# Seven block products, not eight, for three of eight k pairs of the MLP down products

## The reference, cut to what matters

```python
D_MODEL, SEQ, D_FF = 2048, 256, 8192
...
    z = rmsnorm(h, norm2_w) @ mlp_w1
    h = h + jnp.square(jax.nn.relu(z)) @ mlp_w2
    return h
...
    h = rmsnorm(h, final_norm_w)
```

## Time and profile before

| | before |
|---|---|
| median of three runs | 2040.35 us |
| span of the profiled execution | 2038.3 us |
| median less span | 2.05 us |
| TensorE busy | 2028.1 us |
| VectorE busy | 1374.0 us |
| ScalarE busy | 1223.2 us |
| matmuls recorded | 9892 |
| moved by DMA | 375.47 MB, mean 184 GB/s |

### The profile page before, as it was taken

The page is one execution under the profiler, slowest core; times in us unless marked ns, Lnnn a source line. Parts: engine busy times, 40 slices in busy tenths (PEclk is TensorE's granted clock), DMA queues, the critical chain, the costliest instruction groups (busy, mean ns, idle before and its releaser), DMA issues.

```text
span 2038.3 us, 25640 instructions
## 1 busy us (share of the span) xinstructions
PE 2028.1 (100%) x9892; PEld 1715.1 (84%) x9892; DVE 1374.0 (67%) x1822; ACT 1223.2 (60%) x1822; POOL 6.1 (0%) x12
## 2 busy tenths in 40 slices
PE   9999999999999999999999999999999999999998
PEld 8888888888898888888889988888888888888886
DVE  6666565757877777748967567976646646755764
ACT  7666666646566788646576445576436535634744
POOL 0000000000000000000000000000000000000000
PEclk9999999999999999999999999999999999999999
DMA  7666555564555545555555446665666666666664
GB/s 262 213 188 197 169 155 161 179 200 169 204 176 181 173 145 160 187 192 187 189 158 159 145 142 220 195 195 186 200 194 186 201 192 187 191 202 188 188 204 146
DMA packets 211166, 375.47 MB, mean 184 GB/s; under 512 B 13875, under 2 KB 48917, under 8 KB 210518
## 3 DMA queue, kind: packets, MB, share of 16 engines
q1 hardware_dynamic: 211046, 373.85, 58.3%
HBM read 371.71 MB, written 2.10 MB: 183 GB/s over the span
## 4 chain that ended last, share of the span: by engine, by line
PE 69%; ACT 0%; issue 0%; DVE 0%; ACTq 0%
PE acc L550 19%; PE acc L552 19%; PE acc L551 19%; PE acc L956 2%; PE acc L958 2%; PE acc L957 2%; PE acc L801 1%; PE acc L779 1%; PE tp L562 1%; PE tp L801 1%; PE xb L811 1%; PE acc L782 0%; PE acc L825 0%; PE xb L817 0%; PE acc L1078 0%; PE acc L1077 0%
## 5 line engine op out<-in xcount | busy, mean ns | idle before, releaser
L1697 DVE TENSOR_TENSOR wlo<-raw,whi 128x1024 fp32r<-128x1024 f32 x633 | 769.5, 1222 | 503.4 <-ACT whi L1106 500.1
L1106 ACT ACTIVATE whi<-raw 128x1024 fp32r<-128x1024 f32 x633 | 665.8, 1058 | 544.5 <-PE acc L552 494.1
L550 PE MATMUL acc<-whi,both 128*128 128x512 f32 (+1 forms) x976 | 375.9, 385 | 0.4 <-DVE wlo L1702 0.4
L552 PE MATMUL acc<-whi,both 128*128 128x512 f32 (+1 forms) x976 | 374.0, 383 | 0.0
L551 PE MATMUL acc<-wlo,both 128*128 128x512 f32 (+1 forms) x976 | 373.8, 383 | 0.0
L552 PEld LDWEIGHTS acc<-whi,both 128*128 128x128 f32 x976 | 183.2, 188 | 35.9
L550 PEld LDWEIGHTS acc<-whi,both 128*128 128x128 f32 x976 | 183.3, 188 | 35.5 <-DVE wlo L1702 0.8
L551 PEld LDWEIGHTS acc<-wlo,both 128*128 128x128 f32 x976 | 183.3, 188 | 34.7
L550 PE MATMUL acc<-whi,aT 128*128 128x512 f32 x508 | 200.2, 394 | 0.0
L550 PE MATMUL acc<-whi,bT 128*128 128x512 f32 x512 | 199.2, 389 | 0.0
L551 PE MATMUL acc<-wlo,bT 128*128 128x512 f32 x512 | 199.2, 389 | 0.0
(11 more groups left out here) (401 smaller groups left out, 2790.9 us busy)
## 6 DMA issues: line engine op xcount, KB each, us to landing
raw<-in_mlp_w SPq DMA_DIRECT2D x256, 512.0 KB, 4.2
raw<-in_w_in_a SPq DMA_DIRECT2D x128, 512.0 KB, 3.8
raw<-in_w_ple_gate SPq DMA_DIRECT2D x64, 512.0 KB, 4.1
raw<-in_w_in SPq DMA_DIRECT2D x64, 512.0 KB, 3.9
raw<-in_w_in_b SPq DMA_DIRECT2D x40, 512.0 KB, 4.2
raw<-in_w_out_a SPq DMA_DIRECT2D x32, 512.0 KB, 4.3
raw<-in_w_out_b SPq DMA_DIRECT2D x32, 512.0 KB, 4.3
raw<-in_w_out SPq DMA_DIRECT2D x32, 512.0 KB, 4.6
```

The source lines that it names most:

```text
L550: pe.matmul(o, hi[:, kt, tok], whi[:, slot, wc], start=start, stop=False)
L552: mm = pe.matmul(o, lo[:, kt, tok], whi[:, slot, wc], start=False, stop=stop)
L1106: act.activation(whi[:, u % RING, 0:n], raw[:, u % RING, 0:n], ACT.Copy).then_inc(hi_done, 1)
L1697: dve.tensor_tensor(wlo[:, u % RING, 0:n], raw[:, u % RING, 0:n], whi[:, u % RING, 0:n].bitcast(F32), ALU.subtract).then_inc(lo_done, 1)
```

## The change

For q = 0, 1 and 2 (`PAIRED` = 3) the down product takes its output columns in two pairs of chunks, j = 0 and 1, of 1024 columns each. A unit is now one k tile x 1024 columns, so a column pair has 16 units, and two units (a k pair) hold a 2 x 2 block of weights; with the tokens' 2 x 2 blocks (two token tiles, two k tiles) these are eight block products of 128 x 128 x 512. For the k pairs in `FAST` = (0, 2, 4) they are formed as seven products of sums and differences of blocks (Winograd's form of Strassen's algorithm), the other five k pairs as eight.

- **TensorE**: `pair_of_chunks`. The first unit of a fast pair has one product (3 matmuls, into `tp[0]`), the second has two (6, into `acc[0][0]` and `acc[1][0]`), and four (12) follow two units later, from the sums of weights `quad_hi` and `quad_lo`, into `acc[0][1]`, `xb[0]`, `tp[1]` and `xb[1]`. Other units have 12, into all four `acc` banks.
- **VectorE**, sums of weights: `quad_summed` makes four sums of blocks (one instruction on 128 x 1024 with a broadcast operand, two on 128 x 512) and the remainders of the two units (128 x 1024 and 128 x 512; one block of the four is not used by itself). `quad_split` makes the remainder of the four sums (128 x 2048) after ScalarE has rounded them (`quad_rounded`).
- **VectorE**, sums of tokens: `tokens_summed` (four of 128 x 128) and `sums_split` (128 x 512), hooked into the up stages; ScalarE rounds them (`sums_rounded`).
- **VectorE**, sums of products: at units 12 to 15 of a column pair `product_sums`, `more_sums`, `first_tokens` and `last_tokens` combine the shared products in `shared` and add them to x; ScalarE first copies `tp[0]` there. After the hooks the four `acc` banks are added to x, each in one instruction, which count `down_d` up. TensorE's next column pair and next up stage wait on `down_d`.
- The norm's scale is applied to relu and to the square instead of to the x update, and the semaphores of the norms become one. The load of the final gain moves from before out2 to behind up3 on SP.

down3 keeps its eight products. The diff, cut to its core:

```diff
+PAIRED = DFF // D - 1
+FAST = (0, 2, 4)
...
-        st += [Stage(f"up{b}", "mlp_w1_2", 4, deep, 2, CH), Stage(f"down{b}", "mlp_w2_2", 4, deep, 2, CH)]
+        st += [Stage(f"up{b}", "mlp_w1_2", 4, deep, 2, CH), Stage(f"down{b}", "mlp_w2_2", *((2, KT, 1, 2 * CH) if b < PAIRED else (4, deep, 2, CH)))]
...
+        def fast_at(u):
+
+            for q in range(PAIRED):
+                s = S[f"down{q}"]
+                if s.u0 <= u < s.u0 + s.chunks * s.units:
+                    n, uu = divmod(u - s.u0, s.units)
+                    if uu // 2 in FAST:
+                        return (2 * q + n) * len(FAST) + FAST.index(uu // 2), uu % 2
+            return None
+
+        def sums_due(u):
+
+            f = fast_at(u - 3)
+            return f[0] if f and f[1] == 0 else None
+
+        def quarters(u):
+
+            return raw[:, u % RING:u % RING + 2, :].rearrange("p s (i n) -> p (s i) n", n=CH)
...
-            sp.wait_ge(sem("gla_rs"), 1)
-            sp.dma_start(gains[:, :], w["final_norm_w_2"].rearrange("(a b) -> a b", a=1).to_broadcast((P, D))).then_inc(sem("final_in"), 16)
             stage("out2")
             for b in range(DFF // D):
                 stage(f"up{b}")
+                if b == PAIRED:
+                    sp.wait_ge(sem("zs_lo"), PAIRED * len(FAST))
+                    sp.dma_start(gains[:, :], w["final_norm_w_2"].rearrange("(a b) -> a b", a=1).to_broadcast((P, D))).then_inc(sem("final_in"), 16)
                 stage(f"down{b}")
...
+            def pair_of_chunks(q, j):
+
+                s, n = S[f"down{q}"], 2 * q + j
+                begun = set()
+
+                def three(o, a, at, w_hi, w_lo, stop):
+                    a_hi, a_lo = a
+                    pe.matmul(o[:, :], a_hi[at], w_hi, start=o.name not in begun, stop=False)
+                    begun.add(o.name)
+                    pe.matmul(o[:, :], a_hi[at], w_lo, start=False, stop=False)
+                    return pe.matmul(o[:, :], a_lo[at], w_hi, start=False, stop=stop)
+
+                def bank_free(i, t):
+                    if acc[i][t].name in begun:
+                        return
+                    if j == 0:
+                        pe.wait_ge(sem("up_out"), 4 * q + 3 + i)
+                    else:
+                        pe.wait_ge(sem("down_d"), 4 * (n - 1) + 2 * i + t + 1)
+
+                zs, zt = (zs_hi, zs_lo), (ahi, alo)
+                for uu in range(s.units):
+                    u, kp = s.u0 + j * s.units + uu, uu // 2
+                    slot = u % RING
+                    if j == 0 and uu % QT == 0:
+                        pe.wait_ge(sem("split_lo"), MOVED.index((f"z{q}", uu // QT)) + 1)
+                    pe.wait_ge(lo_done, u + 1)
+                    tok = [(slice(None), uu, slice(t * P, (t + 1) * P)) for t in range(TT)]
+                    cols = [slice(i * CH, (i + 1) * CH) for i in range(2)]
+                    if kp in FAST and uu % 2 == 0:
+                        if n == 0:
+                            pe.wait_ge(tp_done, b[0])
+                        else:
+                            pe.wait_ge(sem("p1_out"), n)
+                        mm = three(tp[0], zt, tok[0], whi[:, slot, cols[0]], wlo[:, slot, cols[0]], kp == FAST[-1])
+                    elif kp in FAST:
+                        i = FAST.index(kp)
+                        pe.wait_ge(sem("zs_lo"), q * len(FAST) + i + 1)
+                        bank_free(0, 0)
+                        three(acc[0][0], zt, tok[0], whi[:, slot, cols[0]], wlo[:, slot, cols[0]], False)
+                        bank_free(1, 0)
+                        mm = three(acc[1][0], zs, (slice(None), i, 3), whi[:, slot, cols[1]], wlo[:, slot, cols[1]], False)
+                    else:
+                        last = uu == s.units - 1
+                        for i in range(2):
+                            for t in range(TT):
+                                bank_free(i, t)
+                                mm = three(acc[i][t], zt, tok[t], whi[:, slot, cols[i]], wlo[:, slot, cols[i]], last)
+                            if last and i == 0:
+                                mm.then_inc(sem("down_half"), 1)
+                    mm.then_inc(unit_used, 1)
+                    g = sums_due(u)
+                    if g is not None:
+                        i = g % len(FAST)
+                        kt, last = 2 * FAST[i] + 1, i == len(FAST) - 1
+                        t_hi, t_lo = quad_hi[g % 2], quad_lo[g % 2]
+                        pe.wait_ge(sem("quad_lo"), g + 1)
+                        if n:
+                            pe.wait_ge(sem("pair_sums"), 4 * n)
+                        bank_free(0, 1)
+                        three(acc[0][1], zt, (slice(None), kt, slice(P, 2 * P)), t_hi[:, 3, :], t_lo[:, 3, :], False)
+                        three(xb[0], zs, (slice(None), i, 0), t_hi[:, 0, :], t_lo[:, 0, :], last)
+                        three(tp[1], zs, (slice(None), i, 1), t_hi[:, 2, :], t_lo[:, 2, :], last)
+                        three(xb[1], zs, (slice(None), i, 2), t_hi[:, 1, :], t_lo[:, 1, :], last).then_inc(sem("quad_used"), 1)
...
                         elif q:
-                            pe.wait_ge(sem("down_x0"), 4 * (q - 1) + 3 + j)
+                            pe.wait_ge(sem("down_d"), 8 * (q - 1) + 6 + 2 * j)
...
+            def quad_rounded(u, g):
+
+                act.wait_ge(lo_done, u + 2)
+                act.activation(quad_hi[g % 2][:, :, :], quad[g % 2][:, :, :], ACT.Copy).then_inc(sem("quad_hi"), 1)
...
+                    f = fast_at(u)
+                    if f and f[1] == 0:
+                        act.activation(whi[:, u % RING, 0:CH], raw[:, u % RING, 0:CH], ACT.Copy).then_inc(hi_done, 1)
+                    elif cols == 2 * QHEAD:
...
+                    if sums_due(u) is not None:
+                        quad_rounded(u - 3, sums_due(u))
...
+            def sums_rounded(q, i):
+                act.wait_ge(sem("zs_step"), 3 * (q * len(FAST) + i + 1))
+                act.activation(zs_hi[:, i], zsum[:, :, :], ACT.Copy).then_inc(sem("zs_hi"), 1)
+
+            def first_product_out(n, u):
+
+                act.wait_ge(unit_used, u + 1)
+                if n:
+                    act.wait_ge(sem("pair_x"), 2 * n)
+                act.activation(shared[:, 0, :], tp[0][:, :], ACT.Copy).then_inc(sem("p1_out"), 1)
...
-                        act.activation(zN[:, t, :], acc[(s.c0 + j) % 2][t][:, :], ACT.Relu).then_inc(sem("up_relu"), 1)
+                        act.activation(zN[:, t, :], acc[(s.c0 + j) % 2][t][:, :], ACT.Relu, scale=rs[:, RS["norm2"], t:t + 1]).then_inc(sem("up_relu"), 1)
                 s = S[f"down{q}"]
-                for j in range(4):
+                for j in range(2 if q < PAIRED else 0):
+                    u = s.u0 + j * s.units + 2 * FAST[-1]
+                    along(s, j, join({} if j else z_hi(q, 3), {12: [lambda n=2 * q + j, u=u: first_product_out(n, u)]}))
...
+                    if f:
+                        if f[1]:
+                            quad_summed(u - 1, f[0])
+                        continue
...
+                    if sums_due(u) is not None:
+                        quad_split(sums_due(u))
                 ptr[0] = max(ptr[0], target)
+
+            def quad_summed(u, g):
+
+                slot, sums = u % RING, quad[g % 2]
+                four = quarters(u)
+                dve.wait_ge(hi_done, u + 2)
+                if g >= 2:
+                    dve.wait_ge(sem("quad_used"), g - 1)
+                dve.tensor_tensor(sums[:, 0:2, :], four[:, 0:4:3, :], four[:, 1:2, :].to_broadcast((P, 2, CH)), ALU.add).then_inc(sem("quad_step"), 1)
+                dve.tensor_tensor(wlo[:, slot + 1, :], raw[:, slot + 1, :], whi[:, slot + 1, :].bitcast(F32), ALU.subtract)
+                dve.wait_ge(sem("quad_step"), 2 * g + 1)
+                dve.tensor_tensor(sums[:, 2, :], sums[:, 0, :], four[:, 3, :], ALU.add).then_inc(sem("quad_step"), 1)
+                dve.tensor_tensor(wlo[:, slot, 0:CH], raw[:, slot, 0:CH], whi[:, slot, 0:CH].bitcast(F32), ALU.subtract).then_inc(lo_done, 1)
+                dve.wait_ge(sem("quad_step"), 2 * g + 2)
+                dve.tensor_tensor(sums[:, 3, :], sums[:, 2, :], four[:, 2, :], ALU.add).then_inc(lo_done, 1)
+
+            def quad_split(g):
+
+                dve.wait_ge(sem("quad_hi"), g + 1)
+                dve.tensor_tensor(quad_lo[g % 2][:, :, :], quad[g % 2][:, :, :], quad_hi[g % 2][:, :, :].bitcast(F32), ALU.subtract).then_inc(sem("quad_lo"), 1)
...
+                if q < PAIRED and 2 * c in FAST:
+                    i = FAST.index(2 * c)
+                    return join(turned, {first + 1: [lambda: tokens_summed(q, c, i)]}, halves, {7: [lambda: sums_split(q, i)]})
+                return join(turned, halves)
+
+            def tokens_summed(q, c, i):
+
+                n = 3 * (q * len(FAST) + i)
+                dve.wait_ge(sem("moved"), P // BLK * (MOVED.index((f"z{q}", c)) + 1))
```

(74 more changed lines are left out.)

74 lines of the change are left out of this document (38 added, 36 removed).

## The result

The changed kernel takes 2070.3 us (median of five runs, 2069.63 to 2072.88) against 2039.59 us (five runs of the kernel before beside it): ratio 1.015, 95% interval 1.0137 to 1.0162. That is 30.7 us slower; the forecast was 27.7 us slower (2068).

The account below looks back on a forecast made before the run. TensorE's matmuls bound the kernel; 36.3 us of waits for VectorE less 12.2 us of removed matmuls gave 24.0, plus 1.4 restarts and 2 clock, 27.4 us on 2040.35: 2068 us, range 2055 to 2084.

Parts of the forecast that it names:

- What bounds the kernel: Whole kernel: TensorE, busy 2028.1 of 2038.3 us, sets the end by matmuls times pitch; it waits for nobody.
- what is removed: down0, down1 and down2: 54 matmuls at 0.227 us, 12.24 us, all on the path.
- Prices on VectorE: Durations from rows of the same kind; without a row, the 2048 split at 2.29 us and the broadcast sum at 1.22.
- The places: Column-pair border, next up stage and first pair's start: TensorE waits for VectorE's in-order work, 12.1 us per down stage.
- border of the pairs: First to second column pair: TensorE stands 4.2 us until VectorE has read acc[0][0].
- next up stage: Second column pair to the next up stage: TensorE waits 2.5 us for VectorE's bank reads.
- z product: Up stage to first column pair: TensorE waits 1.8 us for VectorE's work on the last z chunk.
- the second wait at the border: First to second column pair: 0.5 us more for acc[1][0], read two reads later.
- Restarts and clock: Behind the waits: slower restarts another 1.4 us, matmuls at 1.2 GHz 2 us for the three stands.
- the clock falls each time: Rival: 15 to 20 matmuls at 0.427 us after each of three to six falls; 2075 to 2086 us, 15%.
- Loads come late: Rival: a fast pair's successors load only when quad_summed ends, in a tight loop; 2070 to 2080 us, 10%.
- Faster: Rival: VectorE's path to the reads is shorter, waits under 4.08 us per down stage; 2028 us with none, 5%.

Follow-up runs that it names:

- The first experiment: Against the change: all four sums of products of a column pair moved to unit 12, nothing added or removed; 2052.09 us, ratio 1.0061.
- Order, further: Against the change: sums of products at unit 12, last z chunk transposed at units 6 to 9, banks acc[0] read before the last remainder; 2045.80 us, ratio 1.0029.
- the last experiment: Two fast pairs, improved order, first and last k pair by banks; now z's bands and remainder spread over units 0, 3, 8; 2034.44 us, ratio 0.9973 against before.
- the two-pair kernel: The improved order with seven products for two k pairs, FAST = (2, 4), so 36 matmuls removed and not 54; 2045.23 us, ratio 1.0025.

## Why the prediction was right, point by point

- **What bounds the kernel** and **what is removed**: right. TensorE waited for nothing in the MLP before, and 54 matmuls fewer are recorded. VectorE, forecast near 80 us, was busy for 82.3 us in each fast down stage; up1, up2 and up3 took 87.2, 88.6 and 87.2 us for the forecast 87.0, since the slow matmuls behind a stand fall into them.
- **Prices on VectorE**: right, the two without a row too. The split of 2048 lasted 2.29 us, and the broadcast sum of 1024 1.22 us, the rate of an ordinary one:

```profile
L1856 DVE TENSOR_TENSOR quad_lo<-quad,quad_hi 128x2048 fp32r<-128x2048 f32 x16 | 36.6, 2290 | 3.0 <-ACT quad_hi L1193 2.9
...
L1845 DVE TENSOR_TENSOR quad<-raw 128x1024 f32<-128x1024 f32 x15 | 18.4, 1224 | 16.1 <-ACT whi L1212 15.8
```

- **The places**: each of the larger ones was met. From start to start less the usual distance, with the forecast in brackets: border of the pairs 4.27 us (4.2), next up stage 2.52 (2.5), z product 1.83 (1.8), unit 4 1.2 (1.2), unit 6 1.48 (1.5).
- **What was mis-sized there**: the second wait at the border (0.5 us for acc[1][0]) was not there. The matmuls behind the stand ran at half pace, so that the second bank was read before TensorE came to it. The first experiment bears this out: there the clock stayed up, and the second wait stands in each second pair.

```profile
1470.24 0.50 PE L1082 MATMUL acc<-whi,zs_hi 128*128 128x512 f32 x1 [0.18 <-DVE x L2618]
```

  The wait at unit 8 (0.3 us) is below what the view lists: its first matmul came 0.14 us late and the next one 0.08 us. The term was 36.3 us for the waits, their restarts at 0.1 us included; the listed stands measured 33.9.
- **Restarts and clock**: I gave 1.4 + 2 us, and 8.8 us were measured (2.5 + 6.3). The mechanism was right and the size wrong. The weak step is "I put 2 us into the sum for the three stands": my 2.0 us for one fall was near what one costs (eight matmuls in 3.5 us behind the first stand, 1.7 us lost), but I counted it once where it came each time. So the rival "the clock falls each time" was true in its mechanism. Its price of 9 to 20 us was too high, because the clock was low for 3.4 us each time and not for 15 to 20 matmuls, and the three bunched waits at a first pair's start did not make it fall in the change (a closer bunch did once, see "Order, further"). These terms were 5.4 us too small and the waits 2.4 us too large, so the sum of 27.4 us was 3 us short of the 30.5 us that the MLP lost. That the two errors partly cancel is luck; each is small beside the 33.9 us that were found where they had been computed.
- **Loads come late**: not seen at the waits. ScalarE did wait for loads in the MLP in the change (28.6 us in all) and not before, yet TensorE's waits lay where they were computed without it, and as long. No run took the loads' share out by itself.
- **Faster**: the condition of the rival, under 4.08 us of waits per down stage, was not met by the change, which lost 14.2 us per down stage. In the last experiment it is met: with 36 matmuls removed the limit is 2.7 us per stage, and 1.0 us was lost.

What stays open: the short losses in the two-pair kernel (3.9 us outside the listed waits) were not traced to their causes. Three fast pairs with the banks in turn were not tried, so it is not known whether the change as it was meant can be made faster than the kernel before; VectorE is busy there for 81 to 82 us of the 83 us that TensorE's matmuls take. The contention of GpSimd and VectorE was not measured by itself.

## What to carry to other kernels

Before work is put on an engine that is "60% busy", write down its queue between the event that starts it and the read that the bound engine stands for; here that sum, made from rows of the old trace, gave each of the five larger waits within 0.1 us, and reordering alone gave back 24.5 of 31 us. The layout that wants all four accumulating banks at once cost 10 us with eight products everywhere, and nothing once the bound engine filled and released the banks in turn at the borders. And a stand of some 4 us cost 1.6 us on top here, because eight matmuls behind it ran at 1.2 GHz.

## What the runs showed of the hardware that I had not expected

- GpSimd and VectorE, both on two SBUF inputs: VectorE's 2.29 us instruction took 4.47 us, its 1.22 us one 2.31 us. Taking some 2.3 us of sums per k pair off VectorE made the kernel slower by 7 us.
- After a stand the first matmul lasted 0.47 to 0.50 us and not 0.39 at full clock, and up to 0.79 us with the clock down.
- The clock fell after one stand of 2.4 us and not after two others of the same length, and in another kernel once after three waits of 0.59, 0.33 and 1.31 us close behind each other.
